# A state-space layer's chain re-ordered: swapped states by transposes, states read from PSUM, two gated tiles placed among the state products

## What is computed

```python
u = x @ w_in                       # 64 groups of 16 channels
h[t] = lam * h[t-1] + B u[t]       # complex state, 64 per group, diagonal
y = Re(C h) + d_skip * u
y = gelu(y)
val, gate = split(y @ w_glu + b_glu, 2)
return val * sigmoid(gate)
```

## Time and profile before

| | |
|---|---|
| median of 3 runs | 1217.24 us (1217.2 to 1219.03) |
| the profiled execution | 1217.58 us |
| its span, first to last instruction | 1215.8 us |
| mean granted TensorE clock | 0.994 of full |
| TensorE busy | 1172.9 us (96%) |
| VectorE busy | 882.3 us (73%) |
| ScalarE busy | 635.1 us (52%) |
| GpSimd busy | 147.8 us (12%) |
| the S5 layer's last `w_in` product ends | 371 us into the span |
| its gated products run, with `y_turned(1)` and biases between | from 405 us to 452 us |

### The profile page before, as it was taken

How to read it: one execution, slowest core, us unless ns; L and a number is a source line. 1 busy time by engine, 2 the same in 40 slices (tenths; PEclk the granted TensorE clock), 3 DMA queues, 4 the chain that set the end, 5 groups by cost and what they waited for, 6 DMA issues and landing times.

```text
span 1215.8 us, 18920 instructions
## 1 busy us (share of the span) xinstructions
PE 1172.9 (96%) x7362; PEld 1001.8 (82%) x7362; DVE 882.3 (73%) x1412; ACT 635.1 (52%) x1069; POOL 147.8 (12%) x205
## 2 busy tenths in 40 slices
PE   9999999899989999999998999999999999999996
PEld 7887899899966778888877878888878977888885
DVE  6779898989676667666668877666676767766665
ACT  5766454444434456554554545555538654654551
POOL 0640089500091000000000000000010000000000
PEclk9999999999998999999999999999999999999999
DMA  6684365555588455665553647666536433866540
GB/s 230 209 289 156 127 195 169 172 188 181 168 192 250 162 185 187 228 190 192 184 189 135 210 139 252 184 189 195 181 110 221 135 106 118 262 191 191 188 159 35
DMA packets 63825, 220.17 MB, mean 181 GB/s; under 512 B 8052, under 2 KB 9972, under 8 KB 63224
## 3 DMA queue, kind: packets, MB, share of 16 engines
q1 hardware_dynamic: 57080, 202.08, 51.6%
q0 software_dynamic: 5504, 14.95, 4.2%
q10 hardware_dynamic: 1152, 1.93, 0.5%
HBM read 210.28 MB, written 7.60 MB: 179 GB/s over the span
## 4 chain that ended last, share of the span: by engine, by line
PE 86%; DVE 9%; ACT 3%; issue 1%; DVEq 0%; ACTq 0%
PE bank L1585 18%; PE bank L1588 9%; PE bank L1600 9%; PE bank L1606 9%; PE bank L1602 9%; PE bank L1577 6%; PE bank L1579 6%; PE bank L1578 6%; PE bank L1692 4%; PE bank L1637 4%; DVE wlo L964 2%; PE bank L1557 1%; DVE ext L964 1%; DVE x_tm L1022 1%; DVE x_tm L1034 1%
## 5 line engine op out<-in xcount | busy, mean ns | idle before, releaser
L964 DVE TENSOR_TENSOR wlo<-raw,whi 128x1024 fp32r<-128x1024 f32 x227 | 285.8, 1266 | 51.0 <-ACT whi L579 48.7
L579 ACT ACTIVATE whi<-raw 128x1024 fp32r<-128x1024 f32 x227 | 238.9, 1058 | 38.9 <-DMA raw<-in_w 22.8
L964 DVE TENSOR_TENSOR ext<-raw,ext 128x1024 fp32r<-128x1024 f32 x142 | 172.9, 1223 | 33.7 <-ACT ext L579 31.0
L1585 PE MATMUL bank<-xboth,whi 128*128 128x512 f32 x488 | 172.9, 397 | 0.0
L1585 PE MATMUL bank<-xboth,ext 128*128 128x512 f32 x472 | 166.3, 393 | 0.0
L579 ACT ACTIVATE ext<-raw 128x1024 fp32r<-128x1024 f32 x142 | 149.5, 1059 | 20.3 <-DMA raw<-in_w 14.4
L1577 PE MATMUL bank<-xboth,whi 128*128 128x256 f32 x496 | 142.0, 286 | 2.1 <-DVE wlo L964 2.1
L1579 PE MATMUL bank<-xboth,wlo 128*128 128x256 f32 x496 | 140.3, 283 | 0.0
L1578 PE MATMUL bank<-xboth,whi 128*128 128x256 f32 x496 | 140.3, 283 | 0.0
L1588 PE MATMUL bank<-xboth,wlo 128*128 128x256 f32 x488 | 126.3, 279 | 0.0
L1588 PE MATMUL bank<-xboth,ext 128*128 128x256 f32 x472 | 122.5, 280 | 0.0
(11 more groups left out here) (386 smaller groups left out, 2327.7 us busy)
## 6 DMA issues: line engine op xcount, KB each, us to landing
raw<-in_w SPq DMA_DIRECT2D x370, 512.0 KB, 4.2
slot<-in_ln_row POOLq DMA_DIRECT2D x16, 512.0 KB, 5.1
toep<-slot POOLq DMA_DIRECT2D x8, 512.0 KB, 9.2
toepA<-toep SPq DMA_DIRECT2D x2, 1024.0 KB, 8.1
BT<-toep SPq DMA_DIRECT2D x2, 1024.0 KB, 7.9
slot<-in_s_B SPq DMA_DIRECT2D x2, 512.0 KB, 4.8
slot<-in_s_C SPq DMA_DIRECT2D x2, 512.0 KB, 4.4
x_tm<-in_x ACTq DMA_DIRECT2D x1, 512.0 KB, 5.5
```

The source lines that it names most:

```text
L579: nc.scalar.activation(hi_of(c), raw[:, c % RAW, :], ACT.Copy).then_inc(w_hi, 1)
L964: V.tensor_tensor(lo_of(c), raw[:, c % RAW, :], hi_of(c).bitcast(F32), ALU.subtract).then_inc(w_lo, 1)
L1585: return mm(dst[:, :], hi_of(c)[:, kc * P:(kc + 1) * P], xboth[:, kc, :, :].rearrange("p a t -> p (a t)"), start=kc == 0, stop=kc == KC - 1)
```

## The change

Four things, all in the S5 layer.

1. `swapped(j)` is no longer a product with a permutation. ScalarE writes a second copy of the `states_by_n` result with its halves exchanged (`swapped_n`, one buffer, so the copy for quarter j waits for `swapped(j-1)`), and TensorE transposes that into a bank of its own (`sw_bank`: 6, 7, 6, 2), four transposes per quarter.
2. The first multiply of `turned(j)` reads the state from PSUM bank j; the copy to `Ssb` is gone. The wait on `m_st` moves from ScalarE to VectorE, ahead of the scan of quarter 2.
3. ScalarE splits T0+8 before the copies of `u_turned(0)` and `u_turned(1)`, T0+9 after the first two quarters, T0+10 after the last two, T0+11 to T0+13 ahead of `gelu(2)`. VectorE splits T0+8 first, makes `turned(0)` ahead of `u_grouped(1)`, and T0+9 to T0+12 stand between the later quarters, with `y_lo` 0 to 3 ahead of `turned(3)`.
4. TensorE's order: `swapped_back(0)` ahead of `u_turned(2)`, `states_by_n(2)` and `swapped_back(1)` ahead of `u_turned(3)`; `within(0)` after `swapped(2)`, `across(0)` and `y_turned(0)` ahead of `swapped(3)`; `glu(0, 0)`, `within(1)`, `glu(0, 1)` ahead of `swapped_back(2)`, `swapped_back(3)` and `across(1)`; `glu(0, 2)` ahead of `y_turned(1)`.

```diff
@@ -158,6 +158,8 @@
             xboth = inner.enter_context(nc.sbuf_tensor("xboth", [P, KC, 2, SEQ], F32R))
         xhi, xlo = xboth[:, :, 0, :], xboth[:, :, 1, :]
         toepA = sb("toepA", [P, GROUPS // 2, P])
+        swapped_n, = overlay(("swapped_n", [P, HALF], F32))
+        swapped_n = swapped_n[:, :]
         silu = sb("silu", [P, SEQ])
         hval = sb("hval", [P, SEQ])
         with ExitStack() as inner:
@@ -302,7 +304,7 @@
         tp_ld = [sem(f"tp_ld{j}") for j in range(4)]
         u0_sb, u1_sb, uT_ps, uT_sb = sem("u0_sb"), sem("u1_sb"), sem("uT_ps"), sem("uT_sb")
         u2_ld = [sem("u2_ld0"), sem("u2_ld1")]
-        by_n_ps, by_n_sb = sem("by_n_ps"), sem("by_n_sb")
+        by_n_ps, by_n_sb, by_n_sw = sem("by_n_ps"), sem("by_n_sb"), sem("by_n_sw")
         st_ps, st_sb, sw_ps, rot_sb, g_sb, gw_ps, hs_sb = (sem(n) for n in ("st_ps", "st_sb", "sw_ps", "rot_sb", "g_sb", "gw_ps", "hs_sb"))
         y_ps, y_sb, yT_ps, yhi_sb, ylo_sb = (sem(n) for n in ("y_ps", "y_sb", "yT_ps", "yhi_sb", "ylo_sb"))
         glu_ps, sig_sb = sem("glu_ps"), sem("sig_sb")
@@ -333,6 +335,7 @@
 
         turn_t = CT[:, 48:64, :, :].rearrange("p (h g) s c -> p h (g s c)", h=2)
         ybank = [bank[4], bank[5], bank[0], bank[1]]
+        sw_bank = [bank[6], bank[7], bank[6], bank[2]]
         ytbank = bank[4:8] + bank[0:4]
         BTs = BT[:, :, :].rearrange("p g (s c) -> p g s c", s=STEP)
 
@@ -787,11 +790,10 @@
 
                     act.wait_ge(by_n_ps, j + 1)
                     nc.scalar.copy(u_tm[:, j % 2, j // 2 * HALF:(j // 2 + 1) * HALF], bank[4 + j][:, :]).then_inc(by_n_sb, 1)
-
-                def states(j):
-
-                    act.wait_ge(st_ps, j + 1)
-                    nc.scalar.copy(Ssb[:, 16 * j:16 * j + 16, :], bank[j][:, :].rearrange("p (g n) -> p g n", g=16)).then_inc(st_sb, 1)
+                    if j >= 1:
+                        act.wait_ge(sw_ps, j)
+                    nc.scalar.copy(swapped_n.rearrange("p (q h s) -> p q h s", q=4, h=2),
+                                   bank[4 + j][:, :].rearrange("p (q h s) -> p q h s", q=4, h=2)[:, :, ::-1, :]).then_inc(by_n_sw, 1)
 
                 ys = ys2.rearrange("p s (g c) -> p g s c", g=16)
 
@@ -811,35 +813,31 @@
                 hi_to(T0 + 7)
                 u_grouped(0)
                 u_out(1)
+                hi_to(T0 + 8)
                 u_turned(0)
                 u_turned(1)
-                hi_to(T0 + 9)
                 states_by_n(0)
                 states_by_n(1)
-                states(0)
-                states(1)
-                hi_to(T0 + 10)
+                hi_to(T0 + 9)
                 u_grouped(1)
                 u_turned(2)
                 u_turned(3)
                 nc.scalar.preload_act_table(ACT.Gelu_apprx_tanh)
-                act.wait_ge(m_st, 16 * 64)
                 states_by_n(2)
                 states_by_n(3)
-                states(2)
-                states(3)
+                hi_to(T0 + 10)
                 gelu(0)
                 gelu(1)
                 for b in range(0, 4):
                     y_hi(b)
-                gelu(2)
-                gelu(3)
-                hi_to(T0 + KC + 4)
+                hi_to(T0 + KC + 5)
                 act.wait_ge(w_used, T0 + KC)
                 act.wait_ge(ones_set, 1)
                 nc.scalar.activation(one_row, ones_row, ACT.Copy)
                 act.wait_ge(bglu_landed, 16 * 4)
                 nc.scalar.activation(bhi, bglu, ACT.Copy).then_inc(bhi_sb, 1)
+                gelu(2)
+                gelu(3)
                 for b in range(4, 8):
                     y_hi(b)
                 nc.scalar.preload_act_table(ACT.Sigmoid)
@@ -1378,11 +1376,13 @@
                 def turned(j):
                     q = slice(16 * j, 16 * j + 16)
                     c = slice(HALF * j, HALF * (j + 1))
-                    dve.wait_ge(st_sb, j + 1)
-                    step(V.tensor_tensor(rot3, Ssb[:, q, :], cosT[:, q, :], ALU.mult))
+                    dve.wait_ge(st_ps, j + 1)
+                    mark(V.tensor_tensor(rot3, bank[j][:, :].rearrange("p (g n) -> p g n", g=16), cosT[:, q, :], ALU.mult))
                     dve.wait_ge(sw_ps, j + 1)
-                    step(V.tensor_tensor(tmp3, bank[j][:, :].rearrange("p (g n) -> p g n", g=16), sinT[:, q, :], ALU.mult))
+                    step(V.tensor_tensor(tmp3, sw_bank[j][:, :].rearrange("p (g n) -> p g n", g=16), sinT[:, q, :], ALU.mult))
                     step(V.tensor_tensor(rotq, rotq, tmpq, ALU.subtract))
+                    if j == 2:
+                        dve.wait_ge(m_st, 16 * 64)
                     V.tensor_tensor_scan(slot[3][:, c], dec[:, c], rotq, 0.0, ALU.mult, ALU.add).then_inc(g_sb, 1)
                     dve.wait_ge(g_sb, j + 1)
 
@@ -1408,24 +1408,28 @@
                 lo_to(T0 + 7)
                 u_grouped(0)
                 u_out(1)
-                lo_to(T0 + 9)
+                lo_to(T0 + 8)
                 V.memset(ones_row, 1.0).then_inc(ones_set, 1)
                 dve.wait_ge(by_n_ps, 1)
                 dec3 = dec.rearrange("p (g n) -> p g n", g=G)
                 step(V.tensor_copy(dec3, mag8[:, :].unsqueeze(2).to_broadcast([P, G, NBLK])))
                 step(V.memset(dec3[:, :, 0:1], 0.0))
+                turned(0)
                 u_grouped(1)
-                turned(0)
                 turned(1)
                 turned_back(0)
                 turned_back(1)
                 turned(2)
-                turned(3)
-                turned_back(2)
-                turned_back(3)
+                lo_to(T0 + 9)
                 for b in range(0, 4):
                     y_lo(b)
+                lo_to(T0 + 10)
+                turned(3)
+                lo_to(T0 + 11)
+                turned_back(2)
                 lo_to(T0 + KC + 4)
+                turned_back(3)
+                lo_to(T0 + KC + 5)
                 dve.wait_ge(bhi_sb, 1)
                 V.tensor_tensor(blo, bglu, bhi.bitcast(F32), ALU.subtract).then_inc(blo_sb, 1)
                 for b in range(4, 8):
@@ -1965,8 +1969,10 @@
                     ins.then_inc(st_ps, 1)
 
                 def swapped(j):
-                    pe.wait_ge(st_sb, j + 1)
-                    mm(bank[j][:, :], perm, slot[3][:, j * HALF:(j + 1) * HALF], start=True, stop=True).then_inc(sw_ps, 1)
+                    pe.wait_ge(by_n_sw, j + 1)
+                    for q in range(4):
+                        ins = nc.tensor.transpose(sw_bank[j][:, q * P:(q + 1) * P], swapped_n[:, q * P:(q + 1) * P], ident)
+                    ins.then_inc(sw_ps, 1)
 
                 def swapped_back(j):
                     pe.wait_ge(g_sb, j + 1)
@@ -2039,33 +2045,35 @@
                 states_by_n(0)
                 states_by_n(1)
                 states(0)
+                swapped(0)
                 states(1)
-                swapped(0)
                 swapped(1)
+                swapped_back(0)
                 pe.wait_ge(ug0_sb, 2)
                 pe.wait_ge(ug1_sb, 2)
                 u_turned(2)
+                states_by_n(2)
+                swapped_back(1)
                 u_turned(3)
-                swapped_back(0)
-                states_by_n(2)
                 states_by_n(3)
-                swapped_back(1)
                 states(2)
+                swapped(2)
+                within(0)
                 states(3)
-                swapped(2)
+                across(0)
+                pe.wait_ge(g_sb, 3)
+                y_turned(0)
                 swapped(3)
-                within(0)
-                across(0)
-                y_turned(0)
+                pe.wait_ge(ylo_sb, 4)
+                glu(0, 0)
+                within(1)
+                glu(0, 1)
+                pe.wait_ge(g_sb, 4)
                 swapped_back(2)
-                within(1)
                 swapped_back(3)
                 across(1)
-                pe.wait_ge(ylo_sb, 4)
-                glu(0, 0)
-                glu(0, 1)
+                glu(0, 2)
                 y_turned(1)
-                glu(0, 2)
                 glu(0, 3)
                 pe.wait_ge(ylo_sb, KC)
                 for c in range(4, KC):
```

## The result

| | before | after |
|---|---|---|
| median | 1217.22 us (1216.48 to 1219.03, 4 runs) | 1227.16 us (1225.19 to 1230.31, 4 runs) |
| profiled execution | 1217.58 us | 1226.6 us |
| its span | 1215.8 us | 1224.8 us |
| mean granted TensorE clock | 0.994 | 0.989 |

The ratio is 1.008, with an interval from 1.0061 to 1.0098: slower by 0.8%. The forecast was 1222.2 with a range up to 1225.5, so the direction was right and the loss twice as large as forecast, 1.7 us beyond the range.

A forecast was written before the change was run, and what follows sets the result against it. TensorE was taken as the bound, with 86% of the chain, waiting on VectorE in the S5 stretch. Order 1.0 plus clock 3.5 and 0.5 made 5.0 us on 1217.58: 1222.6, as a median 1222.2; range 1216.5 to 1225.5.

The forecast's parts named there:

- Parts 1 and 2 at nothing: In the S5 chain, swapping by transposes and reading states from PSUM were to change the time by nothing.
- The order walked at full clock: Parts 3 and 4 in the S5 chain, priced at full clock: `glu(0,4)` at 418.5 against 417.50, 1.0 us later.
- The clock at +3.5 and +0.5: TensorE's clock lowered about 381 to 392, 3.5 us; a possible second fall from the stand before `across(1)`, 0.5 us.
- the loss at 652: Existing clock fall near 652, 3.5 us at half clock, used to price a second fall: at most some 1.7 us.
- the mark: Start of `glu(0,4)`, 417.50 us before; whatever moves it moves the end as much if TensorE stays dense behind it.
- Rival (b): In the S5 chain the clock stays lowered from 379 to 396: `glu(0,4)` at 424.6, 7.1 us, 1224.4; chance 0.20.
- Rival (a): In the S5 chain the clock holds or falls no longer than before: 1218.2 to 1219.6; chance 0.25.
- Rival (c): TensorE, not VectorE, bounds between `swapped_back(3)` and `across(1)`: `glu(0,4)` at 414.5, 3.0 us earlier, 1214.2; chance 0.12.

The follow-up runs named there:

- e1: Kernel before with parts 1 and 2 alone, all four orders as before: 1219.3 us against 1218.64, ratio 1.0006.
- e9: Changed kernel, order and waits kept, with products nobody reads put into TensorE's waits: 1224.7 us, ratio 1.0036 to the kernel before.
- e10: Kernel before with products nobody reads put into its own TensorE waits: 1217.35 us, ratio 0.9993.
- e3: Changed kernel with the transposes of `states` and `swapped` made as plain products with the identity: 1229.03 us, ratio 1.0087 to the kernel before.
- e2: Changed kernel with permutation products and `Ssb` copies put back, so parts 3 and 4 alone: 1228.78 us, ratio 1.009 to the kernel before.
- e4: Changed kernel with `u_turned(3)` right behind `u_turned(2)` and `swapped_back(1)` behind `states_by_n(3)`: 1225.06 us, ratio 1.0056 to the kernel before.
- e6: Changed kernel with `u_turned(3)` early and `swapped_back(2)`, `swapped_back(3)` ahead of `glu(0,1)`: 1219.57 us, ratio 1.0006 to the kernel before.
- e8: e6 plus splits of T0+11, T0+12 behind `turned_back(3)` and the Gelu table loaded ahead of the `u_turned(2)` copies: 1219.28 us, ratio 1.0002.
- e11: e8 with products nobody reads ahead of `swapped_back(0)` and `glu(0,0)`: 1215.62 us against 1217.76 for the kernel before, ratio 0.9983.
- e12: Changed kernel again, unedited, on the same chip as e7 and e9 to e11: 1228.18 us, ratio 1.0081 to the kernel before.
- e7: Changed kernel with VectorE's splits of T0+11 and T0+12 moved behind `turned_back(3)`: 1225.45 us, ratio 1.0063 to the kernel before.
- e5: Changed kernel with `swapped_back(2)` and `swapped_back(3)` ahead of `glu(0,1)`: 1223.09 us, ratio 1.0033 to the kernel before.

## Why the prediction was right in its direction and too low in its size

**Parts 1 and 2 at nothing: right.** An exchanged copy takes 0.60 where the plain one beside it takes 0.59; the steps of `turned` start at the same spacing, the second 0.1 sooner; e1 is level with before.

**The order walked at full clock: right in its steps, a little low in its sum.** `turned(0)` came at 376.16 (376.0 walked). VectorE waited for `u_turned(3)` ahead of `turned_back(0)`: 2.1 walked at full clock, 2.44 in e9, which has the clock there. The wait at `turned_back(2)` was 2.80 (2.2 walked), the stand at `across(1)` 4.01 (4.0). From `ylo_sb` 4 to `across(1)` 13.75 passed, and 13.6 was walked. The sum for the order was +1.0. No run gives it alone. e9's stretch is 3.2 us longer than before, of which 1.5 lie in e9's own fall at the head (`turned(0)` starts 6.38 behind the first `u_turned`, 4.91 in the changed kernel). That leaves 1.7 us, in the terms of the +1.0. Against e10, which was filled too, it is 3.2, but e10's own fall was only halved. So the term was 0.7 to 2.2 us low. The two executions of e9 at 0.998, 0.8 and 2.1 us over the kernel before, fit the lower figure.

**The clock at +3.5 and +0.5: the step that failed, by its size.** The direction and the place were right: lowered under the short single pieces from 382.3 on, and again around `across(1)`. But I took one long fall ending at 392 and priced what it doubled on the path. In the profile the clock is up again from 385.8 to 389.2, and then down to 396, under `within(0)` (3.64 where 1.8 was the price), and the second fall cost 1.7 (`across(1)` to `glu(0,4)` took 9.96, walked 8.3) where I took 0.5 by the loss at 652. Holding the clock in e9 gave back 4.4 us of the stretch; with the 1.5 of its own fall this makes about 6 us, against 4.0. So the +4.0 for the clock is the term that was mis-sized most. The sum by the profiles is then 1.7 for the order, 5.9 for the clock and 1.3 behind the mark, which I took as unchanged: 8.9 of the 9.0 us of span. About 0.9 of that 1.3 comes from the pooling layer on, where the same thin work met the clock at another moment. This division rests on single profiles; whole times give the clock's part as 5.5 us or more, since e9 still has falls.

**Rival (b)**, a longer fall to 396, came nearest: its mark was 424.6 and the profile has 425.18. This is luck in part. It rightly had the fall go on until `within(0)`, but two of the pieces that it slows, `swapped_back(0)` and `u_turned(2)`, ran at full clock (1.13 and 1.18), and the longer second fall made up for them. Its reason was transposes not counting, and e3 and e2 show the same loss without them. What e4 to e9 support instead is that VectorE's and TensorE's waits for each other thin out TensorE's work. That lowers the clock, and the lower clock lengthens the waits. **Rival (a)** is what e6 and e8 look like in time and clock (down for 6.8 us, as before), but with the waits taken out, which (a) kept. **Rival (c)** named the right switch: in e8 and e11 `across(1)` doesn't wait, TensorE is the bound there, and with the clock held as well (e11) the kernel is faster than before, by 2.1 us where (c) had 3.0, which is still under the 0.2%.

**The range** was too narrow because its upper end was one fall's length with dearer copies. With falls whose place and number differ from run to run, the upper end should have been the whole thin stretch, 379 to 417, at the lower clock.

## What to carry to other kernels

Before work of the next stage is placed in the bottleneck engine's holes, walk what stands behind it on that engine, and who waits for that: here two pieces of about 1 us each (`swapped_back(2)`, `u_turned(3)`) came late and held VectorE up, and putting them first gave back the whole loss (e6). Where two engines wait for each other in turns, count the stretch once at the full and once at the lower clock, and take the second as the upper end of the range. Fill the bottleneck's longest waits with harmless products only after the order is right, and time it: it gave 0.45% where waits were long, 0.19% in the mended order, and nothing measurable in the kernel before.

## What the runs showed of the hardware

The falls of the clock are no fixed property of a program. The same changed kernel, profiled twice, was at the lower level from 382.3 to 385.8, from 389.2 to 396.0 and from 416.5 to 419.9 the first time. The second time it fell at 374.9, 385.1, 402.2 and 415.8, for 3.4 us each. Its times spread over 6.6 us in 6 executions (1224.73 to 1231.36), those of the kernel before, on the same chip, over 4.8 in 23. The Trainium skill ("TensorE: Matmul & The Clock Gate", Part 1: The HAM clock gate) says that at a kernel's start the number of products at the lower clock differs from run to run. The two profiles show the like in the middle of a kernel.

One fall is regular. In all six profiles in which TensorE stands for 2.9 to 4.0 us in front of `across(1)` with nothing put in (the changed kernel, e12, e2, e3, e4, e7), the clock goes down within 1.4 us of the start of `across(1)`, which then takes 2.40 to 3.56 us. In the five without that stand (e5, e6, e8, e9, e11) it doesn't fall there, and `across(1)` takes 1.95 or 1.96. What decides where the other falls begin was not found.

Products that nobody reads hold the clock behind the place where they stand. In e11, 3 of them, placed in two waits, go with a mean granted clock of 1.00 over the 42 us from 378 on, where e8 has 0.92. A fall that began ahead of them (374.8) ran its 3.4 us. In e10 the products put in ahead of `swapped_back(0)` didn't keep the clock from falling at 382.5; it was down for 3.4 us instead of 6.8.
